# Dilated attention: the reciprocal roots of the query and key norms made by GpSimd as a power, none by ScalarE

## Chip, core and metric

One Trainium2 chip, one NeuronCore of it. The metric is the device time of one execution in microseconds; a kernel's time is the median of its runs. Everything is float32.

## The reference, cut to what matters

The program is a two-part model on 512 tokens of width 1024: a first block (two attentions and a mixture of experts), then a second block with a dilated attention layer and a gated linear attention layer. The change touches only the dilated layer (the three outputs are merged by a softmax over `lse`):

```python
def rms_norm(x, g):
    xf = x.astype(jnp.float32)
    y = xf * lax.rsqrt(jnp.mean(xf * xf, axis=-1, keepdims=True) + EPS)
    return (y * g.astype(jnp.float32)).astype(x.dtype)

def dilated_mixer(cols, cos, sin, q_gain, k_gain):
    qkv = cols.reshape(B, S, 3, N_GROUPS_2, A_HEADS, HEAD_DIM)   # 3 dilations, 8 heads of 128
    q = rms_norm(qkv[:, :, 0], q_gain[:, None, :])
    k = rms_norm(qkv[:, :, 1], k_gain[:, None, :])
    v = qkv[:, :, 2]
    q, k = apply_partial_rotary(q, cos5, sin5), apply_partial_rotary(k, cos5, sin5)
    for g, (window, dil) in enumerate(DIL_PAIRS):                # softmax(q k / sqrt(128)) v
        o, lse = dilated_window_attention(q[:, :, g], k[:, :, g], v[:, :, g], dil, window // dil)
    ...
```

## The kernel before, in words

The kernel is one hand-ordered program: each engine has its own instruction list, and semaphores tie them together. Weights stream from HBM through six slots (`wraw`). ScalarE copies each piece to a rounded high part `whi` (line 1054, `feed`), VectorE subtracts to get the low part `wlo` (line 1699, its `feed`), and TensorE multiplies three times for each product (line 2579): high by high, low by high, high by low.

In the dilated stage there are eight heads, and for each head twelve steps `i`: four pieces of the query projection (0 to 3), four of the key's (4 to 7), four of the value's (8 to 11), 384 columns each for three dilations. Between the pieces of head `hd` the attention of head `hd - 1` is worked in four units `r` of three steps (scores, probabilities, output), which `attention_step` spreads over the twelve. So each engine does in one step a bit of projection and a bit of attention.

- Scores: TensorE multiplies (line 3083), VectorE masks and finds the maxima (lines 2271 to 2275, `dil_maxima`, semaphore `att_m`), ScalarE takes Exp (lines 1506, 1508, semaphore `att_p`). Probabilities: TensorE transposes (line 2606). Output: lines 3094, 3096.
- At `q == 3` of query and key, ScalarE squares the projection out of PSUM (line 1550), VectorE writes it with its gain to `qk_t` (line 2325) and sums the squares (line 2331). VectorE then does its `feed` for the step, and line 2338 makes the mean squares `ms`, 128x12: 4 token tiles by 3 dilations. ScalarE takes the Sqrt of those 12 columns (line 1560), and VectorE the reciprocal (line 2346 for a key; 2343 and 2344, with the scale 128 ** -0.5, for a query).
- GpSimd waits for that result (semaphore `qk_rs`), multiplies it in (line 996 for a key: all 1536 columns; line 998 for a query: the first dilation's 512 only, the other two are scaled in the masks of the maxima), applies the rotary in six instructions (lines 857 to 862), and signals `qk_rot`. From the third head on it then merges an earlier head's outputs (lines 989 to 991).
- TensorE waits for `qk_rot` in steps 6 (query) and 10 (key), line 3119, after the second of the step's four token tiles, and transposes `qk_t` (line 2606).

`link` on GpSimd lets an instruction signal and then waits for that signal. Norms are counted by `n`, `n = 2 * hd` for the query and `2 * hd + 1` for the key.

Of the kernel before, what the change touches and what calls it, by code (L numbers as in the profile page):

```python
# [21 lines left out]
ALU = mybir.AluOpType  # L22
ACT = mybir.ActivationFunctionType
AX = mybir.AxisListType

P = 128
T, D = 512, 1024
NT, KD = T // P, D // P
EPS = 1e-6
# [79 lines left out]
def build(nc, A, out):  # L109
    ctx = ExitStack()  # L110
    with ctx:
# [308 lines left out]
        def norm_cols(n):  # L420
            return dict(ss=stat(n), ms=stat(n), rt=stat(n), rs=stat(n))
# [10 lines left out]
        rs_mod4 = stat(16).rearrange("p (t r) -> p t r", t=NT)  # L432
        far_at = stat_at[0]
        qk_n = norm_cols(12)
        q_rs = [stat(12).rearrange("p (t g) -> p t g", t=NT) for _ in range(2)]
        k_rs = stat(12).rearrange("p (t g) -> p t g", t=NT)
        gl_n = norm_cols(32)
# [404 lines left out]
        def _(pool):  # L842
# [142 lines left out]
            def merge(hd):  # L985
# [4 lines left out]
                link(pool.tensor_tensor(near_o, near_o, mg_e[:, 0, :].unsqueeze(2).broadcast_to([P, NT, P]), ALU.mult))  # L990
                pool.tensor_tensor(far_o, far_o, near_o, ALU.add).then_inc(S("merged"), 1)

            for n in range(16):
                pool.wait_ge(S("qk_rs"), n + 1)
                if n % 2:
                    link(pool.tensor_tensor(heads, heads, k_rs.unsqueeze(3).broadcast_to([P, NT, 3, P]), ALU.mult))
                else:
                    link(pool.tensor_tensor(heads[:, :, 0, :], heads[:, :, 0, :],  # L998
                                            q_rs[n // 2 % 2][:, :, 0:1].broadcast_to([P, NT, P]), ALU.mult))
                rope(heads[:, :, :, 0:16], heads[:, :, :, 16:32], cos2, sin2, rtmp, (NT, 3, 16)).then_inc(S("qk_rot"), 1)  # L1000
                if n % 2 == 0 and n >= 4:
                    merge(n // 2 - 2)
# [41 lines left out]
        def _(act):  # L1044
# [479 lines left out]
            for hd in range(9):  # L1524
                for i in range(12):
                    for half in range(2):
                        for k in dil_steps(hd, i, half):
                            unit_step(hd, k)
                        if hd == 8 and i == 6 and half == 0:
                            gated_hi(0, 0, (0, 1))  # L1530
                    nm, q = "qkv"[i // 4], i % 4
                    if hd == 8:
                        if q == 3:
                            gate_out(0, i // 4, silu_sb)
                        merge_exp(hd, i)
                        feed(chunks[CH[f"gate0{THIRDS[0][i // 4]}"]]["first"] + q + SPL)
                        if i == 6:
                            gated_hi(0, 0, (2, 3))
                        continue
                    j = CH[f"{nm}d{hd}"]  # L1540
                    n = 2 * hd + i // 4
                    if q == 3:
                        for t in range(NT):
                            wait_acc(act, j, t)
                            if nm == "v":
                                act.activation(v2[:, hd % 2, t, :], ACC[t][:, 0:384], ACT.Copy, scale=rs_perm[:, t:t + 1]).then_inc(acc_free[t], 1)
                            else:
                                if n:
                                    act.wait_ge(S("qk_red"), NT * n - NT + t + 1)
                                act.activation(sqs[t], ACC[t][:, 0:384], ACT.Square, scale=rs_perm[:, t:t + 1]).then_inc(S("qk_sq"), 1)  # L1550
                    name, dst = (f"dq_{hd}", qT) if i == 6 else (f"dk_{hd}", kT)
                    if i in (6, 10):
                        tcopy(name, 0, in_order(dst[:, hd % 2, 0, :]), by_residue(tb(name, 0)))
                        tcopy(name, 1, dst[:, hd % 2, 1, :], tb(name, 1))
                    merge_exp(hd, i)
                    if n or nm == "v" or q == 3:
                        feed(chunks[j]["first"] + q + SPL)
                    if q == 3 and nm != "v":
                        act.wait_ge(S("qk_ms"), n + 1)
                        act.activation(qk_n["rt"], qk_n["ms"], ACT.Sqrt).then_inc(S("qk_rt"), 1)  # L1560
                    if i in (6, 10):
                        tcopy(name, 2, dst[:, hd % 2, 2, :], tb(name, 2))
            end_phase(act, "ACT")
# [121 lines left out]
        def _(dve):  # L1685
# [576 lines left out]
            def dil_maxima(hd, r):  # L2262

                u = dil_unit(hd - 1, r)
                U, b = u["U"], (hd - 1) % 2
                c = U % 4
                mx = att_mx[:, 2 * c:2 * c + 2]
                near_m, m = u["near"][:, P:P + 1], far_m[b][:, r:r + 1]
                dve.wait_ge(att_s, U + 1)
                for (src, _, _), (to, mask, scale), top_ in zip(u["s"], u["masked"], (near_m, mx[:, 0:1], mx[:, 1:2])):  # L2270
                    ins = dve.tensor_tensor_reduce(to, src, mask, scale, LOW, ALU.add, ALU.max, top_)
                link(ins)
                dve.tensor_scalar(att_nm[:, c:c + 1], near_m, -1.0, None, ALU.mult)
                link(dve.tensor_reduce(m, mx, AX.X, ALU.max))
                dve.tensor_scalar(far_nm[:, c:c + 1], m, -1.0, None, ALU.mult).then_inc(att_m, 1)
# [22 lines left out]
            for hd in range(9):  # L2298
                for i in range(12):
                    for half in range(2):  # L2300
                        for k in dil_steps(hd, i, half):
                            step, r = attention_step(k)
                            if step == "scores":
                                dil_maxima(hd, r)
                            elif step == "probs" and (k != 4 or hd == 8):
                                dil_probs(hd, r)
                        if hd == 8 and i == 6 and half == 0:
                            gated_lo(0, 0, (0, 1))
                    nm, q = "qkv"[i // 4], i % 4
                    if hd == 8:  # L2310
                        merge(hd, i)
                        if q == 3:
                            gate(0, i // 4, silu_sb)
                        feed(chunks[CH[f"gate0{THIRDS[0][i // 4]}"]]["first"] + q + SPL)
                        if i == 6:
                            gated_lo(0, 0, (2, 3))
                        continue
                    j = CH[f"{nm}d{hd}"]
                    n = 2 * hd + i // 4
                    if q == 3 and nm != "v":  # L2320
                        if n:
                            dve.wait_ge(tp_ready, TPU[f"dq_{hd}" if nm == "k" else f"dk_{hd - 1}"] + 3)
                        for t in range(NT):
                            dve.wait_ge(S("qk_sq"), NT * n + t + 1)
                            dve.scalar_tensor_tensor(qk_t[:, t, :].rearrange("p (g c) -> p g c", g=3),
                                                     ACC[t][:, 0:384].rearrange("p (g c) -> p g c", g=3), rs_perm[:, t:t + 1],
                                                     qkg[:, :, i // 4, :], ALU.mult, ALU.mult).then_inc(acc_free[t], 1)
                        if hd and i == 3:
                            dil_probs(hd, 1)
                        for t in range(NT):  # L2330
                            dve.tensor_reduce(qk_n["ss"][:, 3 * t:3 * t + 3], sqs[t].rearrange("p (g c) -> p g c", g=3), AX.X, ALU.add
                                              ).then_inc(S("qk_red"), 1)
                    merge(hd, i)
                    if n or nm == "v" or q == 3:
                        feed(chunks[j]["first"] + q + SPL)
                    if q == 3 and nm != "v":
                        dve.wait_ge(S("qk_red"), NT * n + NT)
                        dve.tensor_scalar(qk_n["ms"], qk_n["ss"], 1.0 / HD, EPS, ALU.mult, ALU.add).then_inc(S("qk_ms"), 1)
                        dve.wait_ge(S("qk_rt"), n + 1)
                        rt_ = qk_n["rt"].rearrange("p (t g) -> p t g", t=NT)  # L2340
                        if nm == "q":
                            rs = q_rs[hd % 2]
                            link(dve.reciprocal(rs, rt_))
                            dve.tensor_scalar(rs, rs, HD ** -0.5, None, ALU.mult).then_inc(S("qk_rs"), 1)  # L2344
                        else:
                            dve.reciprocal(k_rs, rt_).then_inc(S("qk_rs"), 1)
            end_phase(dve, "DVE")
            for c in (1, 2):
                gated_lo(0, c)
# [894 lines left out]
```

## Time and profile before

| | |
|---|---|
| median of 3 runs | 1959.98 us (1958.95 to 1962.04) |
| the profiled execution's own time | 1960.95 us |
| its span, first to last instruction | 1959.3 us, mean granted TensorE clock 0.993 |
| busy: TensorE, its weight loads | 1884.0 us (96%), 1632.4 us (83%) |
| busy: VectorE, ScalarE, GpSimd | 1183.9 (60%), 1033.2 (53%), 358.4 (18%) us |
| chain that ended last, by engine | PE 68%, DVE 16%, DMA 6%, ACT 6% |

In the rows PE is TensorE, PEld its weight loads, DVE VectorE, ACT ScalarE, POOL GpSimd, and L12 is line 12 of the kernel. A busy TensorE is not TensorE at its peak, and idle time of another engine costs nothing unless TensorE waits for what comes after it.

### The profile page before, as it was taken

How to read it: one execution, taken by the hardware profiler on the slowest of the kernel's cores; microseconds unless marked ns; L12 is line 12 of the kernel's file. 1: busy time of each engine (PE TensorE's matmuls, PEld its weight loads, DVE VectorE, ACT ScalarE, POOL GpSimd, SP SyncE). 2: the span in 40 equal slices, each digit the busy share in tenths (PEclk: the TensorE clock that was granted, in tenths of full speed). 3: DMA queues.
4: the chain of work that ended last, by engine and by line, in shares of the span. 5: the costliest groups of instructions: out<-in, count | busy, mean ns of one | idle time of the engine just before them, and what ended most of it. 6: DMA issues, size and time to landing. Idle time of an engine off the chain costs nothing.

```text
span 1959.3 us, 27334 instructions
## 1 busy us (share of the span) xinstructions
PE 1884.0 (96%) x10047; PEld 1632.4 (83%) x10047; DVE 1183.9 (60%) x2466; ACT 1033.2 (53%) x1803; POOL 358.4 (18%) x453
## 2 busy tenths in 40 slices
PE   7999999999999999899999999999999999999998
PEld 7977877777787777688999999999888777777887
DVE  3335388654799999765444554445344635856972
ACT  5654543444688787654544544545443555445441
POOL 1601232010001101032112322133020101411310
PEclk9999999999999999999999999999999999999999
DMA  4511222127699999832323223233243522122231
GB/s 152 142 52 44 65 65 76 44 79 256 225 365 360 366 356 359 290 108 58 89 82 90 81 83 91 83 88 102 86 138 122 166 61 76 55 65 65 66 108 43
DMA packets 187312, 259.44 MB, mean 132 GB/s; under 512 B 14605, under 2 KB 101594, under 8 KB 187178
## 3 DMA queue, kind: packets, MB, share of 16 engines
q1 hardware_dynamic: 178048, 225.56, 35.8%
q0 software_dynamic: 8720, 31.59, 4.3%
q8 instruction: 81, 1.33, 0.3%
q10 hardware_dynamic: 410, 0.52, 0.1%
q14 instruction: 53, 0.43, 0.1%
HBM read 239.24 MB, written 14.16 MB: 129 GB/s over the span
## 4 chain that ended last, share of the span: by engine, by line
PE 68%; DVE 16%; DMA 6%; ACT 6%; issue 2%; POOL 1%; SPq 0%; ACTq 0%; DVEq 0%; POOLq 0%
PE pb L2579 50%; DVE wlo L1699 8%; PE pb L2606 5%; DMA wraw<-w_down 3%; ACT whi L1054 3%; PE pb L2662 2%; PE pb L2675 2%; DMA wraw<-w_up 2%; PE pb L3191 1%; PE pb L2949 1%; DMA wraw<-w_mem_kv 1%; PE pb L3154 1%; DVE AT_lo L2045 1%; PE pb L2838 1%; PE pb L3096 1%
## 5 line engine op out<-in xcount | busy, mean ns | idle before, releaser
L1699 DVE TENSOR_TENSOR wlo<-wraw,whi 128x1024 fp32r<-128x1024 f32 (+4 forms) x430 | 502.9, 1183 | 470.5 <-ACT whi L1054 468.4
L2579 PE MATMUL pb<-whi,AT_hi 128*128 128x512 f32 (+4 forms) x1864 | 724.2, 389 | 7.0 <-DVE arena L2006 2.1
L2579 PE MATMUL pb<-whi,AT_lo 128*128 128x512 f32 (+4 forms) x1864 | 676.8, 363 | 0.0
L2579 PE MATMUL pb<-wlo,AT_hi 128*128 128x512 f32 (+4 forms) x1864 | 675.3, 362 | 0.0
L1054 ACT ACTIVATE whi<-wraw 128x1024 fp32r<-128x1024 f32 (+4 forms) x446 | 440.3, 995 | 331.8 <-PE pb L2579 268.1
L2579 PEld LDWEIGHTS pb<-whi,AT_hi 128*128 128x128 f32 x1864 | 352.2, 189 | 50.4 <-issue 16.9
L2579 PEld LDWEIGHTS pb<-wlo,AT_hi 128*128 128x128 f32 x1864 | 352.6, 189 | 39.3 <-issue 6.5
L2579 PEld LDWEIGHTS pb<-whi,AT_lo 128*128 128x128 f32 x1864 | 351.3, 188 | 39.8
L2606 PE MATMUL pb<-arena 128*128 128x128 f32 (+1 forms) x1044 | 159.5, 278 | 29.0 <-ACT arena L1508 6.3
L2606 PEld LDWEIGHTS pb<-arena 128*128 128x128 f32 (+1 forms) x1044 | 129.3, 146 | 62.8 <-ACT arena L1508 9.5
L2949 PE MATMUL pb<-whi,AT_hi 128*128 128x512 f32 x256 | 105.4, 412 | 2.4 <-DVE AT_lo L2045 1.2
L2949 PE MATMUL pb<-whi,AT_lo 128*128 128x512 f32 x256 | 101.0, 394 | 0.0
L2949 PE MATMUL pb<-wlo,AT_hi 128*128 128x512 f32 x256 | 100.9, 394 | 0.0
L1034 POOL TENSOR_TENSOR arena<-arena 128x256 f32<-128x256 f32 x72 | 66.1, 923 | 187.4 <-ACT arena L1637 176.5
L1090 ACT ACTIVATE arena<-pb 128x512 f32<-128x512 f32 (+2 forms) x89 | 54.7, 669 | 39.3 <-PE pb L2606 39.3
L3191 PE MATMUL pb<-arena 128*128 128x128 f32 (+1 forms) x352 | 56.5, 289 | 10.5 <-ACT arena L1637 3.8
L1637 ACT ACTIVATE arena<-arena 128x512 f32<-128x512 f32 x64 | 39.5, 629 | 51.1 <-DVE arena L2448 38.5
L3191 PEld LDWEIGHTS pb<-arena 128*128 128x128 f32 x352 | 50.3, 192 | 19.2 <-DVE arena L2475 6.2
L1146 ACT ACTIVATE arena<-pb,small 128x64 f32<-128x64 f32 x64 | 20.2, 316 | 87.4 <-PE pb L2675 87.2
L998 POOL TENSOR_TENSOR arena<-arena,small 128x512 f32<-128x512 f32 x8 | 8.4, 1049 | 304.5 <-DVE small L2344 304.5
L2949 PEld LDWEIGHTS pb<-whi,AT_hi 128*128 128x128 f32 x256 | 48.7, 190 | 18.0 <-DVE wlo L1699 7.6
L911 POOL TENSOR_TENSOR wlo<-wraw,whi 128x1024 fp32r<-128x1024 f32 x16 | 38.2, 2390 | 109.8 <-ACT whi L1054 109.8
(347 smaller groups left out, 2585.4 us busy)
## 6 DMA issues: line engine op xcount, KB each, us to landing
wraw<-w_in_a SPq DMA_DIRECT2D x288, 128.0 KB
wraw<-w_gate SPq DMA_DIRECT2D x128, 256.0 KB
wraw<-w_up SPq DMA_DIRECT2D x128, 256.0 KB
wraw<-w_down SPq DMA_DIRECT2D x58, 512.0 KB
wraw<-w_in_b SPq DMA_DIRECT2D x40, 512.0 KB
wraw<-w_in SPq DMA_DIRECT2D x28, 512.0 KB
wraw<-w_mem_kv SPq DMA_DIRECT2D x16, 512.0 KB
wraw<-w_in_a SPq DMA_DIRECT2D x16, 512.0 KB
```

The lines of the kernel that those rows point to most:

```text
L911: pool.tensor_tensor(w_slot(wlo, p, p % SPL), raw_slot(p), w_slot(whi, p, p % SPL).bitcast(F32), ALU.subtract).then_inc(lo_done[p % SPL], 1)
L1034: pool.tensor_tensor(e2, q2, e2, ALU.mult).then_inc(S("gl_q"), 1)
L1054: act.activation(w_slot(whi, p, p % SPL), raw_slot(p), ACT.Copy).then_inc(hi_done, 1)
L1090: act.activation(dst, src, ACT.Copy, scale=scale).then_inc(tp_free[u % 2], 1)
L1637: act.activation(kq[n % 5], kq[n % 5], ACT.Exp).then_inc(S("gl_x"), 1)
L1699: dve.tensor_tensor(w_slot(wlo, p, p % SPL), raw_slot(p), w_slot(whi, p, p % SPL).bitcast(F32), ALU.subtract).then_inc(lo_done[p % SPL], 1)
L2579: mm = pe.matmul(ACC[bank][:, 0:n], a, b, start=kc == 0 and q == 0, stop=i == c["count"] - 1 and kk == per - 1 and q == 2)
L2606: tr = pe.transpose(TP[u % 2][0:b.shape[1], at:at + P], b, ident)
L2662: pe.matmul(SC[U % 2][:, 0:u["kw"]], u["q"], u["k"], start=True, stop=True).then_inc(att_s, 1)
L2675: mm = pe.matmul(TP[tu % 2][:, 0:u["dv"]], pt[:, P * b:P * b + P], u["v"][b], start=b == 0, stop=b == nb - 1)
L2949: mm = pe.matmul(ACC[n % 2].rearrange("p (w f) -> p w f", w=2), a, b, start=k == 0 and m == 0, stop=k == 7 and m == 2)
L3191: mm = pe.matmul(SC[m % 2][:, c0:c0 + rhs.shape[1]], lhs, rhs, start=True, stop=True)
```

## The change

The reciprocal square root leaves ScalarE and VectorE. VectorE's line 2338 now writes, for a query, the sum of squares plus 128 * EPS, and for a key the mean plus EPS, so that the power of minus one half gives the query's scale 128 ** -0.5 with it. GpSimd raises those 12 columns to the power -0.5 (a tensor_tensor instruction with the operation `pow`, its second input one column of -0.5 broadcast), then waits for its own result and goes on as before. The Sqrt of ScalarE and its wait are gone, as are the reciprocal, the scaling and a wait of VectorE. VectorE waits for the previous norm's power before it overwrites `ms`, and, since it no longer writes `q_rs` itself, before the first maxima of a head. GpSimd waits for the old head's maxima (`att_m`) before it overwrites `q_rs`.

```diff
+        neg_half = stat(1)
...
+            power = neg_half.unsqueeze(1).broadcast_to([P, NT, 3])
+            link(pool.memset(neg_half, -0.5))
             for n in range(16):
+                rs = k_rs if n % 2 else q_rs[n // 2 % 2]
+                if n % 2 == 0 and n >= 4:
+                    pool.wait_ge(att_m, AU["dil"] + NT * (n // 2 - 1))
+                pool.wait_ge(S("qk_ms"), n + 1)
+                pool.tensor_tensor(rs, qk_n["ms"].rearrange("p (t g) -> p t g", t=NT), power, ALU.pow).then_inc(S("qk_rs"), 1)
                 pool.wait_ge(S("qk_rs"), n + 1)
...
-                    if q == 3 and nm != "v":
-                        act.wait_ge(S("qk_ms"), n + 1)
-                        act.activation(qk_n["rt"], qk_n["ms"], ACT.Sqrt).then_inc(S("qk_rt"), 1)
...
+                if r == 0:
+                    dve.wait_ge(S("qk_rs"), 2 * hd - 1)
                 dve.wait_ge(att_s, U + 1)
...
                         dve.wait_ge(S("qk_red"), NT * n + NT)
-                        dve.tensor_scalar(qk_n["ms"], qk_n["ss"], 1.0 / HD, EPS, ALU.mult, ALU.add).then_inc(S("qk_ms"), 1)
-                        dve.wait_ge(S("qk_rt"), n + 1)
-                        rt_ = qk_n["rt"].rearrange("p (t g) -> p t g", t=NT)
-                        if nm == "q":
-                            rs = q_rs[hd % 2]
-                            link(dve.reciprocal(rs, rt_))
-                            dve.tensor_scalar(rs, rs, HD ** -0.5, None, ALU.mult).then_inc(S("qk_rs"), 1)
-                        else:
-                            dve.reciprocal(k_rs, rt_).then_inc(S("qk_rs"), 1)
+                        if n:
+                            dve.wait_ge(S("qk_rs"), n)
+                        per = 1.0 if nm == "q" else 1.0 / HD
+                        dve.tensor_scalar(qk_n["ms"], qk_n["ss"], per, per * HD * EPS, ALU.mult, ALU.add).then_inc(S("qk_ms"), 1)
```

## Rows read from the trace of the kernel before

**Rows 1.** The page's part 1: busy time, share of the span, instructions.

```profile
PE 1884.0 (96%) x10047; PEld 1632.4 (83%) x10047; DVE 1183.9 (60%) x2466; ACT 1033.2 (53%) x1803; POOL 358.4 (18%) x453
```

**Rows 2.** Busy time by stage, the dilated stage; columns as in its first line.

```profile
core 0: us, PE busy (x) PEld busy (x) DVE busy (x) ACT busy (x) POOL busy (x), PEclk, DMA share, GB/s
902.00:1400.00 498.00, 488.33 (x2986) 477.36 (x2985) 244.00 (x612) 245.06 (x467) 115.65 (x130) 1.00 0.31 87
```

**Rows 3.** Waits, 900 to 1370 us: total, times, longest.

```profile
POOL arena L998 <- DVE small L2344: 304.5, 8, 53.8
...
POOL arena L996 <- DVE small L2346: 90.3, 8, 14.5
...
ACT small L1560 <- DVE small L2338: 30.2, 16, 2.7
...
PE pb L2606 <- ACT arena L1508: 4.6, 7, 0.9
...
PE pb L2606 <- POOL arena L862: 1.7, 1, 1.7
```

**Rows 4.** Groups by line, ScalarE, 880 to 1400 us: busy, mean ns.

```profile
L1560 ACT ACT_TABLE_LOAD x15 | 19.2, 1283 | 0.3
L1506 ACT ACT_TABLE_LOAD x15 | 19.2, 1283 | 0.3
...
L1560 ACT ACTIVATE small<-small 128x12 f32<-128x12 f32 x16 | 3.4, 214 | 30.2 <-DVE small L2338 30.2
```

**Rows 5.** Timeline of ScalarE, key step of the fourth head: start, duration.

```profile
1105.58 1.28 ACT L1560 ACT_TABLE_LOAD   x1
...
1109.37 0.84 ACT L1054 ACTIVATE whi<-wraw 128x768 fp32r<-128x768 f32 x1 [0.52 <-PE pb L2579]
1110.23 1.28 ACT L1506 ACT_TABLE_LOAD   x1
1113.79 0.51 ACT L1506 ACTIVATE arena<-arena,small 128x256 f32<-128x256 f32 x1 [2.27 <-DVE small L2275]
```

**Rows 6.** Timeline of VectorE, same head, query step and key step.

```profile
1088.36 0.17 DVE L2338 TENSOR_SCALAR small<-small 128x12 f32<-128x12 f32 x1
...
1089.54 1.65 DVE L1699 TENSOR_TENSOR wlo<-wraw,whi 128x768 fp32r<-128x768 f32 x1 [0.29 <-ACT whi L1054]
...
1107.24 0.95 DVE L1699 TENSOR_TENSOR wlo<-wraw,whi 128x768 fp32r<-128x768 f32 x1
1108.10 0.17 DVE L2338 TENSOR_SCALAR small<-small 128x12 f32<-128x12 f32 x1
...
1110.24 2.18 DVE L1699 TENSOR_TENSOR wlo<-wraw,whi 128x768 fp32r<-128x768 f32 x1 [1.47 <-ACT whi L1054]
```

**Rows 7.** Timeline of GpSimd: first head, then the fourth's query and key.

```profile
910.22 0.60 POOL L862 TENSOR_TENSOR arena<-arena 128x192 f32<-128x192 f32 x1
...
1089.33 1.05 POOL L998 TENSOR_TENSOR arena<-arena,small 128x512 f32<-128x512 f32 x1 [36.21 <-DVE small L2344]
1090.46 1.14 POOL L857 TENSOR_TENSOR arena<-arena 128x192 f32<-128x192 f32 x1
...
1093.74 0.60 POOL L862 TENSOR_TENSOR arena<-arena 128x192 f32<-128x192 f32 x1
...
1108.86 2.75 POOL L996 TENSOR_TENSOR arena<-arena,small 128x1536 f32<-128x1536 f32 x1 [10.53 <-DVE small L2346]
1111.69 1.14 POOL L857 TENSOR_TENSOR arena<-arena 128x192 f32<-128x192 f32 x1
...
1114.97 0.60 POOL L862 TENSOR_TENSOR arena<-arena 128x192 f32<-128x192 f32 x1
```

**Rows 8.** Timeline of TensorE's transposes: first head, then the fourth.

```profile
911.20 1.03 PE L2606 MATMUL pb<-arena 128*128 128x128 f32 x8
...
931.02 1.09 PE L2606 MATMUL pb<-arena 128*128 128x128 f32 x8 [1.69 <-POOL arena L862]
...
1096.00 1.03 PE L2606 MATMUL pb<-arena 128*128 128x128 f32 x8
...
1114.93 0.66 PE L2606 MATMUL pb<-arena 128*128 128x128 f32 x4 [0.62 <-ACT arena L1508]
...
1117.54 1.04 PE L2606 MATMUL pb<-arena 128*128 128x128 f32 x8
```

**Rows 9.** Groups by line, GpSimd, the whole span: busy, mean ns.

```profile
L996 POOL TENSOR_TENSOR arena<-arena,small 128x1536 f32<-128x1536 f32 x8 | 22.0, 2754 | 90.3 <-DVE small L2346 90.3
...
L990 POOL TENSOR_TENSOR arena<-arena,small 128x512 f32<-128x512 f32 x8 | 8.3, 1041 | 0.0
```

## Prediction

> **What bounds the kernel now.** The first view is the page's table of engines: TensorE is busy 96% of the span, so time is won or lost only where TensorE stands idle [rows 1]. All sixteen edited norms (a query norm and a key norm for each of eight heads) lie in the dilated stage, so the second view is the table of stages: from 902 to 1400 us TensorE is busy 488.3 of 498.0 us at full granted clock, ScalarE 245 and VectorE 244 us, GpSimd 116 us [rows 2]. The whole stage holds under 10 us of TensorE idleness. The third view, the waits, says who ends it: GpSimd waits long for its scales (304.5 and 90.3 us), which costs nothing by itself; TensorE waits 4.6 us in seven times for the softmax exponentials of line 1508, and once 1.7 us for GpSimd's last rotary instruction, line 862 [rows 3]. Those are the only idle stretches that the change can touch from either side.
>
> **ScalarE's side: what is removed.** The stage has 15 table loads before the Sqrt of line 1560 and 15 before the next Exp of line 1506, 1.283 us each, 38.5 us in all, and sixteen Sqrt [rows 4]. The timeline of one head shows where they lie. The Sqrt load runs at 1105.58, ahead of the wait for the mean squares. The Exp load runs at 1110.23 to 1111.51, and then ScalarE still waits 2.27 us for VectorE until 1113.79 [rows 5]. Both loads fill time in which ScalarE would wait anyway, so I price their removal at nothing; were that cover gone, one load would cost up to 1.28 us a head. The weight copy of line 1054 at 1109.37 waits for TensorE's piece [rows 5], so it doesn't move either. The Trainium skill (ScalarE: Activation LUTs, What ACT_TABLE_LOAD costs) gives 1283 ns a load, which the trace repeats, and adds a drain of about 1380 ns, which no row here shows. By that page's figure the thirty switches would be worth about 80 us of ScalarE time; by the idle time behind each load, nothing.
>
> **VectorE's side.** The reciprocal, and for a query the scaling and the wait for ScalarE's root disappear; ScalarE's own 16 waits for the mean squares, 30.2 us, go as well [rows 3]. In the key step VectorE next waits for ScalarE's weight copy until 1110.24 [rows 6], so nothing is gained there. The two added VectorE waits (on the previous norm's power before the mean squares are overwritten, and before a head's first maxima) ask for powers made a third of a head earlier: nothing, unless the power takes many microseconds. Queued behind them would be the maxima and the weight differences of line 1699, and behind those TensorE.
>
> **GpSimd's side: what is added, and what it delays.** Before, from the end of line 2338 (1108.10 + 0.17 = 1108.27) to the key multiplication of line 996 at 1108.86 there are 0.59 us; for a query from 1088.53 to 1089.33, 0.80 us [rows 6, 7]. After, that stretch is a signal of 0.09, the power D, and a signal to itself of 0.08 (the gaps ahead of line 857 [rows 7]): 0.17 + D. So the key multiplication comes D - 0.42 later, the query's D - 0.63.
>
> A late key multiplication is not hidden, because of how line 996 and line 1699 meet. Line 1699 alone takes 0.95 us; begun at 1110.24 while line 996 ran until 1111.61, it took 2.18 and ended at 1112.42, 0.81 after line 996. The query step repeats this: line 998 ends at 1090.38, line 1699 at 1091.19, again 0.81 later. In turn line 857 takes 1.14 us while line 1699 ends [rows 6, 7]. The one that comes second stands still until the first is done. The maxima are queued behind line 1699, the exponentials behind them, and TensorE's transposes behind those: 1112.42 + 2.51 = 1114.93, where TensorE has idled 0.62 us [rows 8]. Hence the price of a key step is the shift of line 996 itself, D - 0.42, as long as line 996 still starts ahead of 1110.24, that is for D under 1.80. The Trainium skill (SBUF — State Buffer, Who interferes with whom) calls this an exclusive lock between GpSimd and a VectorE instruction with two SBUF inputs, held for the whole instruction; the trace agrees, with its 0.81 us in both places. Were bandwidth split instead, the seven key steps of the sum below would cost about half, and the sum be 4.3 us in place of 7.1.
>
> Query step: the rotary (lines 857 to 862) ends at 1094.34 and TensorE takes its result at 1096.00 [rows 7, 8]. The rotary took 3.88 us from 1090.46, of which 0.73 was line 857 standing still until 1091.19, so 3.15 by itself. At worst the power keeps line 1699 out as the other tensor operations of GpSimd do: power from 1088.62 to 1088.62 + D, line 1699 for 0.81, line 998 for 1.05, the signal 0.08, the rotary 3.15, and one more line 1699 in its midst, 0.81, make 1094.52 + D. So nothing for D up to 1.48, and D - 1.48 above. Key rotary: 1115.57 against 1117.54 [rows 7, 8]; both move by D - 0.42, so its 1.97 us of slack stay.
>
> **The power's own time D** stands in no row. Below: an ordinary operation on 12 elements. From 1536 elements in 2754 ns and 512 in 1041 ns [rows 9] the slope is 1.67 ns an element and the fixed part 0.18 us, with them 0.20 us. Above: 2.75 us, the whole of line 996, which is 128 plain operations for each of the 12 elements. [...] It is nearer to the upper row than to a plain product; I count 50 plain operations an element, 0.18 + 12 x 50 x 0.00167 = 1.2 us. This is the weakest number here.
>
> **Sum.** Key steps of the seven heads after the first: 7 x (1.2 - 0.42) = 5.5 us. First head: its key result is awaited directly by TensorE (the 1.69 us at 931.02), so +0.8; its query rotary ends at 910.82 against 911.20, a slack of 0.38 [rows 7, 8], which a delay of 0.57 overruns by 0.2, and by 1.0 if another line 1699 comes between: I take 0.8. Together 7.1 us. On the profiled execution's 1960.95 us that gives 1968.1; the median of the runs is 1959.98, 0.97 lower, so **1967 us**. At D = 0.20 the seven heads give 7 x (-0.22) = -1.5 us; at 1.80 they give 7 x (1.38 + 0.32) = 12, which holds the query steps, and with 3 for the first head 15.
>
> **Rivals.**
> - *A short power*, D up to 0.85: -1.5 to 3.9 us, 1958.5 to 1963.8. For it: only 12 elements. Chance 0.28.
> - *The order turns over*, D from 1.88 to 3.5: line 996 is no longer ahead of line 1699. Line 1699 runs as soon as the power ends, so the 0.62 us idle shrinks or goes; but line 996 starts after it, at 1109.17 + D, and its rotary (2.75 + 0.08 + 3.15, and one more line 1699, 0.81) ends at 1115.96 + D, where TensorE, without its idle, wants it at 1116.92. Net D - 1.58 for a key, D - 1.48 for a query, so 7 x (2D - 3.06) and 3 to 6 us for the first head: +10 at D = 2, +26 at 3, +34 at 3.5, so 1970 to 1994; at the bound D = 2.75 it is +22. Chance 0.16.
> - *A long power*, D over 3.5, if the elements of a partition group are worked one by one: by the same terms 7 x (2D - 3.06) and some 10 for the first head, for D = 6 +73 us, 2033 us. No row speaks for or against. Chance 0.14.
> - *Faster*: line 1699 gets ahead of line 996 and the key rotary is still in time, which needs D above 1.80, a power that doesn't keep line 1699 out, and a key rotary that ends 1 us sooner than counted above. Then the 0.62 us of seven heads goes: -4.3 us, 1955.7. Against it: every GpSimd tensor operation in these rows did keep it out. Chance 0.05.
> - *Table loads on the path*: if the order of ScalarE's queue passed its 38.5 us on, 1921 us. Rows 5 speak against it. Chance 0.02.
>
> **Numbers.** The forecast, D from 0.85 to 1.88, has 0.35, and its own range is 1964 to 1975. 0.2% is 3.9 us, about what a measurement of this kernel tells from no change. Faster: 0.05 + 0.02 = 0.07. Same: 0.28. Slower: 0.35 + 0.16 + 0.14 = 0.65. The range goes from 1955, the faster case, to 1990, the turned order up to D = 3.3; outside lie the long power, the table case and the end of the turned order, 0.19.
>
> **What the new profile would show.** No table load in the stage but the first; the power on GpSimd 16 times, with D; line 996 D - 0.42 later behind line 2338; line 1699 of the key step ending 0.81 after line 996, and TensorE's idle ahead of line 2606 grown from 0.62 to about 1.4 us in seven heads. Wrong would be: D outside 0.85 to 1.88, line 1699 ahead of line 996, or TensorE waiting for line 862 in heads after the first.

## The result and the profile after

The changed kernel takes 1969.64 us, the kernel before beside it 1961.01 us: ratio 1.0044, 95% interval 1.0027 to 1.0060. It is slower by about 8.6 us. Forecast were 1967 us and a rise of 7.1.

The page of the kernel after, parts 1 and 4 (engines; the chain that ended last by engine):

```profile
PE 1887.2 (96%) x10047; PEld 1633.5 (83%) x10047; DVE 1156.6 (59%) x2442; ACT 993.5 (50%) x1757; POOL 400.0 (20%) x470
...
PE 60%; DVE 17%; POOL 7%; DMA 6%; ACT 5%; issue 3%; SPq 0%; ACTq 0%; DVEq 0%; POOLq 0%
```

ScalarE is 40 us less busy than in [rows 1], VectorE 27 us less, GpSimd 42 us more, and GpSimd's share of the last chain went from 1% to 7%. TensorE executes the same 10047 multiplications; of the 11.4 us that its span grew (1959.3 to 1970.7), 3.2 are busy time and 8.2 are idle time.

The waits of the kernel after from 900 to 1370 us (total, times, longest), which answer to [rows 3], and the transposes of the last head's key, which lie behind 1370 us here:

```profile
POOL small L1001 <- DVE small L2348: 320.1, 16, 33.7
...
PE pb L2608 <- POOL arena L863: 10.5, 8, 3.0
...
1380.93 1.09 PE L2608 MATMUL pb<-arena 128*128 128x128 f32 x8 [1.70 <-POOL arena L863]
```

The seven waits for the exponentials (4.6 us before) are gone, and TensorE waits 10.5 + 1.7 = 12.2 us for GpSimd's last rotary instruction (1.7 before): 5.9 us more waiting in all. (A last wait of 1.67 us for exponentials behind the eighth head is the same in both kernels.) To leave out what other stages did, the tables below also give the time from the start of the first mean squares to the start of the last. The view of one line shows it, before (line 2338) and after (line 2348), with the power (line 1001):

```profile
L2338 DVE TENSOR_SCALAR small<-small x16: 165/167/173, 904.7 to 1357.8; 128x12 f32<-128x12 f32 x16
```

```profile
L2348 DVE TENSOR_SCALAR small<-small x16: 165/166/170, 910.2 to 1370.4; 128x12 f32<-128x12 f32 x16
L1001 POOL TENSOR_TENSOR small<-small x16: 2272/2272/2311, 910.5 to 1370.6; 128x12 f32<-128x12 f32 x16
```

That is 453.1 us before and 460.2 after: 7.1 us of the difference lie between the sixteen norms. Heads in the middle of the stage repeat exactly, so three of them (from the start of one key multiplication to the same instruction three heads on) can be laid side by side, before and after (the stretch, its length, then busy time and instructions of TensorE, its weight loads, VectorE, ScalarE and GpSimd, the granted clock, the DMA share and GB/s):

```profile
1046.41:1233.70 187.29, 184.70 (x1145) 181.90 (x1144) 93.62 (x243) 94.42 (x183) 45.95 (x51) 1.00 0.31 85
```

```profile
1057.28:1246.70 189.42, 185.35 (x1145) 181.71 (x1144) 83.85 (x235) 78.67 (x165) 59.24 (x58) 1.00 0.30 84
```

For the same 1145 multiplications the changed kernel needs 2.13 us more, 0.71 a head. The waits above make 1.3 us of that (3.2 against 1.9); 0.65 is busy time of TensorE, which these views don't explain. (The changed kernel's profiled execution took 1972.38 us, 11.4 over that of before. Its first mean squares stand 5.5 us later, ahead of any power: 4.2 us of it were there at the end of the experts' stage, and the rest is a granted clock of 0.50 from 900 to 903 us, against 1.00 in the kernel before. The kernels of the experiments that carry the edit or a half of it have their first mean squares anywhere from 901.9 to 910.2 us, so this shift isn't put down to the edit.)

The power takes 2.27 us, not 1.2. The same head as in [rows 5 to 8], timelines of the kernel after, GpSimd, VectorE and TensorE in that order (start, duration):

```profile
1098.11 2.27 POOL L1001 TENSOR_TENSOR small<-small 128x12 f32<-128x12 f32 x1 [33.66 <-DVE small L2348]
1100.46 1.05 POOL L1006 TENSOR_TENSOR arena<-arena,small 128x512 f32<-128x512 f32 x1
...
1104.99 0.61 POOL L863 TENSOR_TENSOR arena<-arena 128x192 f32<-128x192 f32 x1
...
1118.08 2.27 POOL L1001 TENSOR_TENSOR small<-small 128x12 f32<-128x12 f32 x1 [9.19 <-DVE small L2348]
1120.43 3.12 POOL L1004 TENSOR_TENSOR arena<-arena,small 128x1536 f32<-128x1536 f32 x1
...
1127.02 0.59 POOL L863 TENSOR_TENSOR arena<-arena 128x192 f32<-128x192 f32 x1
```

```profile
1098.55 0.96 DVE L1704 TENSOR_TENSOR wlo<-wraw,whi 128x768 fp32r<-128x768 f32 x1 [0.58 <-ACT whi L1062]
...
1117.84 0.17 DVE L2348 TENSOR_SCALAR small<-small 128x12 f32<-128x12 f32 x1
1119.98 0.96 DVE L1704 TENSOR_TENSOR wlo<-wraw,whi 128x768 fp32r<-128x768 f32 x1 [1.98 <-ACT whi L1062]
```

```profile
1105.66 1.10 PE L2608 MATMUL pb<-arena 128*128 128x128 f32 x8
...
1123.88 0.60 PE L2608 MATMUL pb<-arena 128*128 128x128 f32 x4
1127.66 1.10 PE L2608 MATMUL pb<-arena 128*128 128x128 f32 x8 [1.05 <-POOL arena L863]
```

In the key step the order has turned over, against the forecast. The weight difference (now line 1704) begins at 1119.98, ahead of the key multiplication (line 1004), and takes its plain 0.96 us instead of 2.18. The maxima and exponentials are in time, and the transposes at 1123.88 carry no idle time (0.62 before). But the multiplication stands behind the difference (3.12 us against 2.75), the rotary ends at 1127.61, and TensorE idles 1.05 us for it. In the query step TensorE takes the rotary's result 0.06 us after it is there (1105.60, 1105.66); there were 1.66 us of slack.

### The profile page after: what moved, and what is told of

The parts are those of the page before. It is cut to its first block, busy times and chain, and to the rows that moved or that the text cites. A ratio compares the mean times of both kernels' runs of the same rounds, so it can differ in the third digit from the quotient of the medians.

```text
span 1970.7 us, 27311 instructions
## 1 busy us (share of the span) xinstructions
PE 1887.2 (96%) x10047; PEld 1633.5 (83%) x10047; DVE 1156.6 (59%) x2442; ACT 993.5 (50%) x1757; POOL 400.0 (20%) x470
## 4 chain that ended last, share of the span: by engine, by line
PE 60%; DVE 17%; POOL 7%; DMA 6%; ACT 5%; issue 3%; SPq 0%; ACTq 0%; DVEq 0%; POOLq 0%
PE pb L2581 44%; DVE wlo L1704 8%; PE pb L2608 5%; DMA wraw<-w_down 2%; ACT whi L1062 2%; POOL small L1001 2%; DMA wraw<-w_up 2%; PE pb L2664 2%; PE pb L2677 2%; PE pb L3193 1%; DVE small L2338 1%; POOL arena L1004 1%; PE pb L2951 1%; DVE arena L2332 1%; DMA wraw<-w_mem_kv 1%
## 5 line engine op out<-in xcount | busy, mean ns | idle before, releaser
L1704 DVE TENSOR_TENSOR wlo<-wraw,whi 128x1024 fp32r<-128x1024 f32 (+4 forms) x430 | 485.5, 1143 | 512.6 <-ACT whi L1062 509.7
L2608 PE MATMUL pb<-arena 128*128 128x128 f32 (+1 forms) x1044 | 161.2, 280 | 36.3 <-POOL arena L863 12.2
L1001 POOL TENSOR_TENSOR small<-small 128x12 f32<-128x12 f32 x16 | 36.4, 2276 | 320.1 <-DVE small L2348 320.1
L947 POOL DMA_INDIRECT x_moe<-arena x7 | 18.2, 2604 | 209.5 <-DVE arena L2156 209.5
```

Of the source, the lines that this page charges most:

```text
L1001: pool.tensor_tensor(rs, qk_n["ms"].rearrange("p (t g) -> p t g", t=NT), power, ALU.pow).then_inc(S("qk_rs"), 1)
L1704: dve.tensor_tensor(w_slot(wlo, p, p % SPL), raw_slot(p), w_slot(whi, p, p % SPL).bitcast(F32), ALU.subtract).then_inc(lo_done[p % SPL], 1)
L2608: tr = pe.transpose(TP[u % 2][0:b.shape[1], at:at + P], b, ident)
```

## Experiments

All ratios are to the kernel before, run on the same chip. "Norms" is the time from the first to the last mean squares in the profiled execution.

| kernel | median, us | ratio (95% interval) | norms, us |
|---|---|---|---|
| before | | 1 | 453.1 |
| after | 1969.64 | 1.0044 (1.0027 to 1.0060) | 460.2 |
| 1 product for power | 1961.70 | 1.0001 (0.9990 to 1.0012) | 453.8 |
| 2 power twice | 2031.31 | 1.0360 (1.0338 to 1.0382) | 518.3 |
| 3 Sqrt put back beside it | 1970.61 | 1.0048 (1.0030 to 1.0066) | 461.9 |
| 4 mean squares earlier | 1968.17 | 1.0037 (1.0018 to 1.0057) | 459.1 |
| 5 queries only | 1964.74 | 1.0016 (1.0001 to 1.0031) | 456.3 |
| 6 keys only | 1967.94 | 1.0034 (1.0020 to 1.0048) | 460.5 |
| 7 rotary ahead of power | 1950.49 | 0.9939 (0.9921 to 0.9957) | 447.2 |
| 8 rotary first, no power | 1963.68 | 1.0015 (1.0002 to 1.0028) | 455.7 |

**1. A plain product in the power's place.**

```diff
-                pool.tensor_tensor(rs, qk_n["ms"].rearrange("p (t g) -> p t g", t=NT), power, ALU.pow).then_inc(S("qk_rs"), 1)
+                pool.tensor_tensor(rs, qk_n["ms"].rearrange("p (t g) -> p t g", t=NT), power, ALU.mult).then_inc(S("qk_rs"), 1)
```

> The power is replaced by a plain product of the same 12 columns, so the norms' values are not the reference's; everything else is the changed kernel. In the changed kernel the power took 2.27 us. Theory A, the length of GpSimd's chain is the cost: the plain product takes about 0.2 us, the key multiplication starts some 0.2 us sooner behind the mean squares than in the kernel before, TensorE's idle ahead of the probability transposes is 0.4 instead of 0.62 us, and the time is 0 to 3 us under the kernel before (ratio 0.9985 to 1.000). Rival B, the added waits and signals cost: the ratio stays at about 1.004.

Ratio 1.0001. Waits of TensorE, and the key step on GpSimd and on VectorE:

```profile
PE pb L2608 <- ACT arena L1516: 3.0, 7, 0.7
...
PE pb L2608 <- POOL arena L863: 1.5, 1, 1.5
```

```profile
1111.84 0.21 POOL L1001 TENSOR_TENSOR small<-small 128x12 f32<-128x12 f32 x1 [10.76 <-DVE small L2348]
1112.12 2.75 POOL L1004 TENSOR_TENSOR arena<-arena,small 128x1536 f32<-128x1536 f32 x1
```

```profile
1111.59 0.17 DVE L2348 TENSOR_SCALAR small<-small 128x12 f32<-128x12 f32 x1
1113.73 1.95 DVE L1704 TENSOR_TENSOR wlo<-wraw,whi 128x768 fp32r<-128x768 f32 x1 [1.97 <-ACT whi L1062]
```

Everything that the change moved is still moved, and the 8.6 us are gone: the power's duration is the cost, not the waits and signals, as far as an interval of about 2 us either way can tell. The plain product takes 0.21 us (0.20 was forecast), the multiplication stands 0.23 us nearer to the mean squares than before (0.36 us behind their end in place of 0.59), the difference ends 0.81 us behind it (1115.68 against 1114.87), and TensorE's seven idle stretches for the exponentials are 3.0 us, 0.43 each. The time is no lower than before, though: three heads take 187.80 us against 187.29, with 0.24 us less idle and 0.75 us more busy time of TensorE. So up to about 0.2 us a head, 1.2 us in all, may belong to something that the edit adds besides the power; the ratio can't tell that from nothing.

**2. The power twice.**

```diff
+                link(pool.tensor_tensor(rs, qk_n["ms"].rearrange("p (t g) -> p t g", t=NT), power, ALU.pow))
                 pool.tensor_tensor(rs, qk_n["ms"].rearrange("p (t g) -> p t g", t=NT), power, ALU.pow).then_inc(S("qk_rs"), 1)
```

> The power is made twice in a row, each awaited, with the same result. Theory A: both the key's and the query's result come 2.35 us later than in the changed kernel, and since TensorE already waits for both, all of it shows: 8 x 4.7 = 38 us over the changed kernel, ratio to the kernel before about 1.023. If the power is mostly hidden and something else costs the 8 us, the ratio stays under 1.012.

Ratio 1.036, 70 us over the kernel before and 62 over the changed one, where 38 were expected. Waits of TensorE from 895 to 1440 us, three heads laid out as above, and the stretch behind the fourth head's key wait:

```profile
PE pb L2609 <- POOL arena L863: 47.8, 16, 5.1
```

```profile
1071.46:1286.59 215.13, 197.85 (x1145) 194.04 (x1144) 86.41 (x234) 79.06 (x166) 71.86 (x64) 0.93 0.26 74
```

```profile
1150.00:1156.00 6.00, 6.00 (x24) 5.90 (x25) 0.00 (x0) 1.72 (x3) 0.00 (x0) 0.53 0.01 3
```

The waits are theory A's: 47.8 us in sixteen, 35.6 over the changed kernel's 12.2, against 38 expected. The rest is TensorE's clock. Three heads take 25.7 us more than in the changed kernel for the same 1145 multiplications: 13.2 are idle time and 12.5 are busy time, at a mean granted clock of 0.93 in place of 1.00. After TensorE has idled 3.27 us for a key its clock is 0.53 from 1150 to 1156 us, that is mostly at the lower level of 1.2 GHz; after a query's 2.25 us it is 0.50 from 1125 to 1128. In the changed kernel the 1.05 us a head leave it at 1.00. The expectation left that out.

**3. The Sqrt and its table loads put back, result unused.**

```diff
+                    if q == 3 and nm != "v":
+                        act.wait_ge(S("qk_ms"), n + 1)
+                        act.activation(qk_n["rt"], qk_n["ms"], ACT.Sqrt).then_inc(S("qk_rt"), 1)
...
+                            dve.wait_ge(S("qk_rt"), n)
```

(The last line is one more wait of VectorE, for the previous norm's root, before it overwrites `ms`.)

> The changed kernel with ScalarE's Sqrt of the mean squares, its wait and so its table loads put back, the result used by nobody. Theory A: the loads lie in ScalarE's waits, the time is the changed kernel's within 2 us, ratio to the kernel before 1.003 to 1.006. Rival C, the removed loads gave back several us that the power then ate: the ratio rises to 1.008 or more.

Ratio 1.0048, against 1.0044 of the changed kernel: the same. The groups of ScalarE show that all thirty loads were there:

```profile
L1568 ACT ACT_TABLE_LOAD x15 | 19.2, 1283 | 0.3
L1514 ACT ACT_TABLE_LOAD x15 | 19.2, 1283 | 0.3
```

38.5 us of ScalarE's time can be put in or taken out without a measurable effect here; an effect under about 3 us would stay inside the intervals. The norms' time differs by 1.7 us in one profiled execution each, but three heads by 0.08 (189.50 against 189.42).

**4. The mean squares ahead of the step's weight difference on VectorE.**

```diff
-                    if n or nm == "v" or q == 3:
-                        feed(chunks[j]["first"] + q + SPL)
                     if q == 3 and nm != "v":
...
                         dve.tensor_scalar(qk_n["ms"], qk_n["ss"], per, per * HD * EPS, ALU.mult, ALU.add).then_inc(S("qk_ms"), 1)
+                    if n or nm == "v" or q == 3:
+                        feed(chunks[j]["first"] + q + SPL)
```

> VectorE makes the mean squares ahead of the step's weight difference, not behind it, so the power starts 0.8 to 0.9 us sooner. Theory A: TensorE's wait for the key rotary falls from 1.05 to about 0.2 us a head and the query's goes, 8 to 9 us under the changed kernel, ratio to the kernel before 0.999 (0.997 to 1.001). Rival B: no change against the changed kernel, 1.004.

The expected gain is missing: 1.0037, within the changed kernel's interval, as rival B had it. Key step, GpSimd, VectorE, TensorE:

```profile
1111.67 2.91 POOL L1001 TENSOR_TENSOR small<-small 128x12 f32<-128x12 f32 x1 [8.46 <-DVE small L2346]
1114.66 3.21 POOL L1004 TENSOR_TENSOR arena<-arena,small 128x1536 f32<-128x1536 f32 x1
```

```profile
1111.50 0.95 DVE L1704 TENSOR_TENSOR wlo<-wraw,whi 128x768 fp32r<-128x768 f32 x1
1114.31 0.96 DVE L1704 TENSOR_TENSOR wlo<-wraw,whi 128x768 fp32r<-128x768 f32 x1 [1.85 <-ACT whi L1062]
```

```profile
1122.00 1.09 PE L2608 MATMUL pb<-arena 128*128 128x128 f32 x8 [1.07 <-POOL arena L863]
```

The power did start earlier, but the weight difference of the same step began just ahead of it (1111.50), and the power took 2.91 us in place of 2.27. The multiplication then met the next difference (1114.31) and took 3.21. So 0.64 us of the start that was won went into the power and 0.09 into the multiplication; TensorE idles 1.07 us as before.

**5 and 6. One half each.** In 5 the power is taken only for `n % 2 == 0` and keys go by Sqrt and reciprocal; in 6 only for `n % 2 == 1`, the other way round. Of 5:

```diff
+                if n % 2 == 0:
+                    pool.wait_ge(S("qk_ms"), n + 1)
+                    pool.tensor_tensor(rs, qk_n["ms"].rearrange("p (t g) -> p t g", t=NT), power, ALU.pow).then_inc(S("qk_rs"), 1)
```

> Queries by the power on GpSimd, keys by Sqrt and reciprocal as in the kernel before. Theory A, from the changed kernel's idle stretches: queries cost 1.2 us in the first head and 0.2 us in each of the others, keys nothing, so 2 to 3 us over the kernel before, ratio 1.0013 (1.000 to 1.003).

> Keys by the power, queries by Sqrt and reciprocal. Theory A: a key costs 1.3 us in the first head, 0.43 in the next six (1.05 of idle for the rotary in place of 0.62 for the exponentials), 0.8 in the last: 4.7 us over the kernel before, ratio 1.0024 (1.001 to 1.004), more than the queries alone. Rival B, the added waits: both halves cost the same.

Ratios 1.0016 and 1.0034, both inside their ranges; together 1.0050, against 1.0044 for both at once. Waits of TensorE in 5, from 895 to 1400 us (the kernel before has 6.3 us in eight times and 1.7 us in one there):

```profile
PE pb L2615 <- ACT arena L1517: 6.3, 8, 1.7
PE pb L2615 <- POOL arena L863: 2.8, 2, 1.7
```

and in 6:

```profile
PE pb L2613 <- POOL arena L863: 11.1, 8, 3.0
...
PE pb L2613 <- ACT arena L1097: 1.6, 6, 0.3
```

Keys cost about twice what queries do by the medians, as theory A has it, but the intervals overlap, so the times alone don't refute rival B. The traces do: three heads take 188.04 us in 5 and 190.33 in 6, against 187.29 before, so 0.25 us a head for queries and 1.01 for keys. The key half alone is dearer than both halves at once (0.71); in it TensorE also waits 0.3 us a head, 1.6 in all, for ScalarE's copies of the transposes, which theory A had not in it. So the two halves don't simply add.

**7. The rotary ahead of the power.** The rotation and the scale of a row can be exchanged, so GpSimd can rotate the unscaled columns while VectorE still sums their squares. It needs scratch of its own, since `rtmp` holds two of the four tiles of squares then.

```diff
+        rope_tmp = view(top[0], 768)
...
+                for t in range(NT):
+                    wait_read(pool, f"{'qk'[n % 2]}d{n // 2}", t)
+                link(rope(heads[:, :, :, 0:16], heads[:, :, :, 16:32], cos2, sin2, rope_tmp, (NT, 3, 16)))
...
-                rope(heads[:, :, :, 0:16], heads[:, :, :, 16:32], cos2, sin2, rtmp, (NT, 3, 16)).then_inc(S("qk_rot"), 1)
+                m.then_inc(S("qk_rot"), 1)
```

(`m` is the multiplication, of line 1009 or 1011.)

> The changed kernel with GpSimd's rotary ahead of the power: it works on the unscaled columns as soon as VectorE has written them, with scratch of its own, and the power and the multiplication follow. The same result up to rounding. Theory A: the key's chain is rotary to about 1 us behind the mean squares, power 2.27, multiplication 2.75, done 2 us ahead of TensorE; the power leaves line 1704 of the next step free, so the exponentials are in time as well. TensorE's idle for both (1.05 and 0.62 us a head) goes, and the first head's: 5 to 7 us under the kernel before, ratio 0.9968 (0.995 to 0.9985).

Ratio 0.9939 (0.9921 to 0.9957), 10.6 us under the kernel before and about 19 under the changed one: the version that beats both. Key step, GpSimd, VectorE, TensorE:

```profile
1101.74 0.54 POOL L860 TENSOR_TENSOR arena<-arena 128x192 f32<-128x192 f32 x1 [8.09 <-DVE arena L2337]
...
1105.69 2.27 POOL L1006 TENSOR_TENSOR small<-small 128x12 f32<-128x12 f32 x1
1108.04 2.75 POOL L1009 TENSOR_TENSOR arena<-arena,small 128x1536 f32<-128x1536 f32 x1
```

```profile
1106.33 0.96 DVE L1709 TENSOR_TENSOR wlo<-wraw,whi 128x768 fp32r<-128x768 f32 x1 [1.25 <-ACT whi L1067]
```

```profile
1110.24 0.60 PE L2613 MATMUL pb<-arena 128*128 128x128 f32 x4
1112.79 1.03 PE L2613 MATMUL pb<-arena 128*128 128x128 f32 x8
```

The chain is done at 1110.79, 2.0 us ahead of TensorE; the difference runs whole inside the power; neither transpose has idle time ahead of it. The norms' time is 5.9 us under the kernel before, as expected. The time as a whole fell by more than the 5 to 7 us, to below the expected range. The profiled executions differ by 9.4 us: 5.9 between the norms, 2.5 behind the last mean squares, where the last head's wait for the exponentials (0.89 us) goes too, and 1.0 ahead of the first. What gave the rest isn't settled.

**8. The same exchange without the power**, on the kernel before.

```diff
+                for t in range(NT):
+                    wait_read(pool, f"{'qk'[n % 2]}d{n // 2}", t)
+                link(rope(heads[:, :, :, 0:16], heads[:, :, :, 16:32], cos2, sin2, rope_tmp, (NT, 3, 16)))
                 pool.wait_ge(S("qk_rs"), n + 1)
...
-                rope(heads[:, :, :, 0:16], heads[:, :, :, 16:32], cos2, sin2, rtmp, (NT, 3, 16)).then_inc(S("qk_rot"), 1)
+                m.then_inc(S("qk_rot"), 1)
```

> The kernel before (Sqrt and reciprocal) with the same reordering of rotary and multiplication. Theory A with the lock of line 996 against the weight difference: the multiplication now starts at about the same time as before or 0.7 us later, behind the rotary and still ahead of the weight difference, so TensorE's idle for the exponentials stays or grows to 1.3 us a head, less the first head's 1.7: ratio 1.000 (0.999 to 1.003). If the reordering alone is what helps, 0.997.

Ratio 1.0015 (1.0002 to 1.0028), inside the expected range. Key step, GpSimd, VectorE, TensorE:

```profile
1108.23 2.75 POOL L1001 TENSOR_TENSOR arena<-arena,small 128x1536 f32<-128x1536 f32 x1
```

```profile
1108.91 2.88 DVE L1704 TENSOR_TENSOR wlo<-wraw,whi 128x768 fp32r<-128x768 f32 x1 [0.83 <-ACT whi L1059]
```

```profile
1114.30 0.66 PE L2611 MATMUL pb<-arena 128*128 128x128 f32 x4 [0.76 <-ACT arena L1513]
```

The multiplication still starts ahead of the difference, which takes 2.88 us and ends 0.81 us behind it (1111.79 against 1110.98), and the exponentials are late by 0.76 us. TensorE also waits 2.5 us in seven times for ScalarE (line 1518) ahead of the scores, which the expectation had not in it. The order of the two decides; the exchange alone gains nothing. In 7 it is the power that holds the multiplication back until the difference is through.

**9. The power's duration by size**, extra instructions on scratch columns behind the merge of head 1.

```diff
+                if n == 6:
+                    for _ in range(2):
+                        for m in (1, 3, 6, 12, 24):
+                            link(pool.tensor_tensor(scratch[:, 0:m], probe[:, 0:m], neg_half.broadcast_to([P, m]), ALU.pow))
+                        for m in (1, 12, 24):
+                            link(pool.tensor_tensor(scratch[:, 0:m], probe[:, 0:m], neg_half.broadcast_to([P, m]), ALU.mult))
```

> The changed kernel with two rounds of extra instructions on scratch columns, on GpSimd in its idle time behind the merge of head 1: the power on 1, 3, 6, 12 and 24 columns and the plain product on 1, 12 and 24. The power of 12 columns takes 2.27 us in the changed kernel. Theory: a fixed part as a plain product has (0.18 us) and about 0.17 us a column, so 0.35, 0.7, 1.2, 2.27 and 4.3 us; the product 0.2 us in all three. Rival: mostly a fixed part, over 1.5 us for one column.

The two rounds take 22 us, more than GpSimd's idle time there: the next key norm is late, TensorE idles 12.8 us for it, and the one execution took 1984.58 us against 1962.28 for the kernel before. Only the durations are used. Groups of GpSimd (line 1016 the power, line 1018 the product; the last number before the idle time is the mean in ns), the two sizes whose rounds agree:

```profile
L1016 POOL TENSOR_TENSOR small<-small 128x12 f32<-128x12 f32 x2 | 4.5, 2266 | 0.2
L1016 POOL TENSOR_TENSOR small<-small 128x1 f32<-128x1 f32 x2 | 1.1, 555 | 0.1
L1018 POOL TENSOR_TENSOR small<-small 128x12 f32<-128x12 f32 x2 | 0.4, 209 | 0.2
```

For 3, 6 and 24 columns they don't agree (0.85 and 1.50, 1.56 and 1.32, 4.16 and 4.53 us), and VectorE's timeline says why: each of the longer ones began while a weight difference (line 1712) was running. The undisturbed ones, the disturbed one of 3 columns, and the difference beside it:

```profile
1107.72 0.85 POOL L1016 TENSOR_TENSOR small<-small 128x3 f32<-128x3 f32 x1
1112.64 4.16 POOL L1016 TENSOR_TENSOR small<-small 128x24 f32<-128x24 f32 x1
1118.37 1.50 POOL L1016 TENSOR_TENSOR small<-small 128x3 f32<-128x3 f32 x1
1119.95 1.32 POOL L1016 TENSOR_TENSOR small<-small 128x6 f32<-128x6 f32 x1
```

```profile
1118.20 0.96 DVE L1712 TENSOR_TENSOR wlo<-wraw,whi 128x768 fp32r<-128x768 f32 x1 [1.98 <-ACT whi L1070]
```

The undisturbed durations, 0.56, 0.85, 1.32, 2.27 and 4.16 us, lie on one line within 0.02 us: 0.39 us and 0.157 us a column. The theory's line was right in form, with the fixed part twice as long as taken (0.18) and the column somewhat shorter; that column is 94 times the product's 1.67 ns [rows 9]. The rival of a mostly fixed power is out. With 0.39 us fixed, six columns take 1.32 us, not half of the 2.27.

## Why the prediction came true, and where it didn't

- **ScalarE's removed loads at nothing**: shown, by experiment 3, within its interval.
- **The added waits at nothing**: shown within about 2 us, by experiment 1, which keeps them all; its trace leaves room for 0.2 us a head.
- **The power's own time**: the step that failed. "I count 50 plain operations an element" gave 1.2 us; it is 2.27, which is 104. No row or run gives the 50. The bounds 0.20 and 2.75 held.
- **Price of a key step, the shift D - 0.42 as long as line 996 is ahead**: the mechanism is shown where it applies, in experiments 1 and 8 (0.81 us behind GpSimd's instruction both times; in 1 the multiplication came 0.23 us sooner and TensorE's idle shrank by 0.19 a head, where split bandwidth would have given half of the shift). No run has a power between 0.21 and 2.27 us, so the forecast's own case was never measured. In the changed kernel it doesn't apply: with 2.27 us the order turned over, the rival that had 0.16, for which the prediction said 1970 to 1994 us. Idle time ahead of the probability transposes didn't grow to 1.4 us; it went, and 1.05 us for the rotary came, 0.43 net in heads 2 to 7 and 0.81 in the last (1.70 in place of 0.89).
- **The rival's own sum** is too high: at 2.27 it gives 7 x 1.48 = 10.4 us and some 3.5 for the first head, 14, against 7.1 between the norms and 8.6 in all. Its key term D - 1.58 says 0.69 where 0.43 was measured, its query term D - 1.48 says 0.79 where a head's period shows 0.22 (63.09 - 62.45 us from one query multiplication to the next, less 0.43) and experiment 5 shows 0.25. Both terms rest on the power keeping line 1699 out. It doesn't, once it has begun: lines at 1098.55 and 1119.98, and 1106.33 in experiment 7, start inside a power and take 0.96 us.
- **First head**: 0.8 for the key and 0.8 for the query were forecast; the idle stretches are 2.99 against 1.69 us, and 1.17 against none, 2.5 in all.
- **So the total** of 7.1 was right by luck, by two errors that offset each other: the power twice as long as taken, and a price that stops rising with it when the order turns. By the prediction's own signs (D outside 0.85 to 1.88, line 1699 ahead of line 996, TensorE waiting for line 862 in later heads) it was wrong in all three; only the size was right.

The rule of the Trainium skill (SBUF — State Buffer, Who interferes with whom) that whichever begins first keeps the shared pair for the whole instruction holds here for GpSimd's multiplications: VectorE's difference ends 0.81 us behind them in the four places read (two in [rows 6, 7], experiments 1 and 8). For the power the runs differ from it: VectorE's difference, begun 0.44 us after the power, was not held up, while a power begun 0.17 us after the difference was held up by 0.64 (experiment 4) or 0.65 (experiment 9).

## What to carry to other kernels

Before an operation is moved to an idle engine, count how long the chain through it becomes and what slack its reader has; that the old engine gets 38 us back is worth nothing if it was waiting. Where instructions of two engines exclude each other, what decides is which of the two begins first, so a shift of a microsecond can pay or cost. A longer one can even be cheaper: by the price D - 0.42 a power of 1.2 us would cost 0.78 us a head, the one of 2.27 us cost 0.43 in a key step; the former is an estimate, not a run. Work that doesn't need the late value (here the rotary) belongs ahead of it in the queue: that turned a loss of 0.4% into a gain of 0.6%.

## What was not expected of the hardware

- A power of 128x12 on GpSimd takes 2.27 us, the product of the same shape 0.21; over 1 to 24 columns the power takes 0.39 us and 0.157 us a column.
- VectorE's two-input subtraction, begun 0.37 us or more after a power began, takes its plain 0.96 us (0.37 beside the 3 columns at 1107.72 of experiment 9, 0.44 and 1.90 in the changed kernel, 0.64 in experiment 7), though GpSimd's products hold it up. That the power is done with its reads by then would fit; no run tests it.
- TensorE's clock: in experiment 2, with two idle stretches a head of 2.2 to 3.3 us, the granted clock averaged 0.93 over three heads, and the loss in them (25.7 us over the changed kernel) was twice the added idle time (13.2).
- VectorE's mean squares of 128x12 took 0.57 us in all sixteen norms of experiments 7 and 8, where GpSimd's rotary runs beside them, against 0.17 in the other kernels. The cause wasn't tested.
